# U and V rows of an expert slot fetched as one 8 KB row, and V rows added by VectorE and GpSimd instead of TensorE

## The reference

```python
best, pos = lax.top_k(cand, PEER_TOPK)
idx = jnp.take_along_axis(cand_idx, pos, axis=-1).reshape(T, PEER_HEADS * PEER_TOPK)
gate = jax.nn.softmax(best, axis=-1).reshape(T, PEER_HEADS * PEER_TOPK)
u_g = jnp.take(u_tab, idx, axis=0)
v_g = jnp.take(v_tab, idx, axis=0)
act = jax.nn.gelu(jnp.einsum('ted,td->te', u_g, xb).astype(jnp.float32)) * gate
return jnp.einsum('te,ted->td', act.astype(xb.dtype), v_g)
```

## Time and profile before

| | before |
|---|---|
| median of 3 runs | 3112.09 us (3095.13 to 3122.34) |
| the profiled execution | 3106.81 us, of which the span is 3105.0 us |
| PE busy | 2791.0 us (90%) |
| DVE busy | 1816.3 us (58%) |
| POOL busy | 1598.9 us (51%) |
| ACT busy | 699.8 us (23%) |
| DMA | 1006.77 MB, mean 324 GB/s |

### The profile page before, as it was taken

The page is one execution under the profiler, slowest core; times in us unless marked ns, Lnnn a source line. Parts: engine busy times, 40 slices in busy tenths (PEclk is TensorE's granted clock), DMA queues, the critical chain, the costliest instruction groups (busy, mean ns, idle before and its releaser), DMA issues.

```text
span 3105.0 us, 33154 instructions
## 1 busy us (share of the span) xinstructions
PE 2791.0 (90%) x11642; PEld 1607.6 (52%) x11642; DVE 1816.3 (58%) x4187; ACT 699.8 (23%) x1340; POOL 1598.9 (51%) x1334
## 2 busy tenths in 40 slices
PE   6999989688899979966699999999989999999997
PEld 4656647433334445534455555555555565555552
DVE  5331124775788746887466765555676755565552
ACT  4111122110104556657111111111111111111110
POOL 2111213274665544655566655565665756565654
PEclk9999999899999999988899999999999999999999
DMA  4332254397999999999999999999999999999997
GB/s 152 112 107 72 89 204 149 132 368 268 366 365 353 385 351 370 374 344 401 389 376 393 392 389 380 388 382 381 378 376 387 378 396 386 381 398 389 397 373 300
DMA packets 341676, 1006.77 MB, mean 324 GB/s; under 512 B 32295, under 2 KB 110887, under 8 KB 338952
## 3 DMA queue, kind: packets, MB, share of 16 engines
q0 software_dynamic: 184320, 671.17, 56.6%
q1 hardware_dynamic: 155464, 308.32, 28.1%
q10 hardware_dynamic: 1728, 25.17, 1.9%
HBM read 958.13 MB, written 46.40 MB: 324 GB/s over the span
## 4 chain that ended last, share of the span: by engine, by line
PE 50%; DMA 15%; issue 7%; DVE 4%; POOL 3%; SPq 1%; ACT 1%; another core or an unknown queue 0%; POOLq 0%; DVEq 0%; ACTq 0%
PE job_ps L1649 16%; PE v_ps L1673 7%; DMA v_rows<-in_peer_v,row_t 6%; PE wide_ps L128 4%; PE wide_ps L129 4%; PE wide_ps L130 4%; PE wide_ps L687 4%; PE job_ps L687 3%; DMA arena<-in_peer_ut 3%; DMA u_row<-in_peer_u,row_u 2%; PE gate_ps L687 2%; DMA arena<-in_peer_v 2%; DVE u_row L1908 1%; POOL u_row L1541 1%; POOL v_rows L1556 1%
## 5 line engine op out<-in xcount | busy, mean ns | idle before, releaser
L1556 POOL DMA_INDIRECT v_rows<-in_peer_v,row_t x622 | 705.7, 1135 | 718.0 <-PE v_ps L1673 561.6
L1908 DVE CUSTOM_DVE_ANT_0 u_row<-u_row,x_tile 128x1024 f32<-128x1024 f32 x640 | 776.3, 1219 | 295.2 <-DMA u_row<-in_peer_u,row_u 264.5
L1541 POOL DMA_INDIRECT u_row<-in_peer_u,row_u x640 | 758.1, 1185 | 289.0 <-issue 190.7
L1649 PE MATMUL job_ps<-arena 128*128 128x512 f32 x1536 | 702.7, 605 | 36.0 <-DVE arena L1968 23.8
L1649 PEld LDWEIGHTS job_ps<-arena 128*128 128x128 f32 x1536 | 288.7, 193 | 392.1 <-issue 339.0
L1673 PE MATMUL v_ps<-v_rows,picked 128*32 128x512 f32 x2488 | 368.0, 621 | 62.8 <-DMA v_rows<-in_peer_v,row_t 52.1
L128 PE MATMUL wide_ps<-x_hi,uw_lo 128*128 128x384 f32 x1024 | 375.4, 367 | 13.4 <-DVE uw_lo L1945 13.4
L129 PE MATMUL wide_ps<-x_lo,uw_hi 128*128 128x384 f32 x1024 | 343.9, 336 | 0.0
L130 PE MATMUL wide_ps<-x_hi,uw_hi 128*128 128x384 f32 x1024 | 343.8, 336 | 0.0
L957 POOL TENSOR_TENSOR exact<-arena,exact 128x1024 fp32r<-128x1024 f32 x48 | 116.3, 2427 | 434.3 <-ACT exact L699 434.3
L1784 ACT ACTIVATE uw_hi<-arena 128x1024 fp32r<-128x1024 f32 x128 | 135.1, 1056 | 720.8 <-DMA arena<-in_peer_ut 629.1
(11 more groups left out here) (302 smaller groups left out, 3060.5 us busy)
## 6 DMA issues: line engine op xcount, KB each, us to landing
arena<-in_peer_ut SPq DMA_DIRECT2D x128, 512.0 KB
arena<-in_peer_v SPq DMA_DIRECT2D x128, 512.0 KB
hand<-tmp_gates SPq DMA_DIRECT2D x32, 768.0 KB
tmp_gates<-arena ACTq DMA_DIRECT2D x10, 2048.0 KB
arena<-in_w_in SPq DMA_DIRECT2D x32, 512.0 KB, 3.7
hand<-in_w_in SPq DMA_DIRECT2D x32, 512.0 KB
x_tile<-tmp_xn SPq DMA_DIRECT2D x80, 128.0 KB
u_row<-in_peer_u,row_u POOLq DMA_INDIRECT x640
```

What stands on the lines that cost most here:

```text
L1541: pool.indirect_dma_start(u_row[n % NU][:], None, dram["peer_u"], bass.IndirectOffsetOnAxis(row_u[g % 2][:, e:e + 1], 0)).then_inc(u_in[n ...
L1556: pool.indirect_dma_start(v_row[b], None, dram["peer_v"], bass.IndirectOffsetOnAxis(row_t[g % 3][:, t:t + 1], 0)).then_inc(v_in[b], 16)
L1649: last = pe.matmul(job_ps[q % 2][:], actd[g % 2][:, jj, d * P:(d + 1) * P], vw[j % NO][:, half * 512:(half + 1) * 512], start=jj == 0, sto ...
L1908: dve.tensor_tensor_reduce(out=u_row[n % NU][:], in0=u_row[n % NU][:], in1=xb[h_ % 2][:], scale=1.0, scalar=0.0, op0=ALU.mult, op1=ALU.add ...
```

## The change

1. The host lays U and V side by side in one table `peer_uv` of 16,384 rows of 8 KB. One indirect DMA (`fetch`) brings 128 rows of 8 KB into one of 7 buffers `row`, and holds U and V for one expert slot of 128 tokens. `fetch_u`, `fetch_v`, the transposes of row numbers and gates and the reordering of tokens go; `xb` is one tile, loaded once per gathered tile (5 loads of 512 KB).
2. `pick`, `turn_act`, `keep_act`, `weigh` and `quad` go. For each slot, ScalarE does gelu of one column, multiplies it by the gate (one column), and scales the right half of V in place (512 wide). Three beats after the dot, VectorE does `add_side`: left half of V times the weight, added to `h`. GpSimd does `add_rest`: the scaled right half, added to `h`, seven slots behind the fetch, just before it reuses that buffer.
3. The dense V matmuls keep their sums in six PSUM banks over all 128 steps (`start=j == 0, stop=j == P - 1`); `sum_dense` runs six times at the end instead of 192 times. `vw` has 4 buffers instead of 6, `actd` holds two single steps.
4. One slot per beat all through: the dense pass starts at beat 240 and takes 3.046 beats a step. 

```diff
-            def fetch_u(n):
+            def fetch(n):
                 g, e = n // P, n % P
                 if e == 0:
                     pool.wait_ge(rows_u_done, g + 1)
-                if n >= NU:
-                    pool.wait_ge(dot_done, n - NU + 1)
-                pool.indirect_dma_start(u_row[n % NU][:], None, dram["peer_u"],
-                                        bass.IndirectOffsetOnAxis(row_u[g % 2][:, e:e + 1], 0)).then_inc(u_in[n % NU], 16)
+                if n >= NR:
+                    pool.wait_ge(added_side, n - NR + 1)
+                    pool.wait_ge(added_rest, n - NR + 1)
+                pool.indirect_dma_start(row[n % NR][:], None, dram["peer_uv"],
+                                        bass.IndirectOffsetOnAxis(row_u[g % 2][:, e:e + 1], 0)).then_inc(row_in[n % NR], 16)
+
+            def add_rest(n):
+                g, e = n // P, n % P
+                pool.wait_ge(scaled, n + 1)
+                if e == 0:
+                    pool.wait_ge(h_in[g % 2], 16 * (g // 2 + 1))
+                if n:
+                    pool.wait_ge(added_rest, n)
+                rest = h[g % 2][:, SIDE:D]
+                pool.tensor_tensor(rest, rest, row[n % NR][:, D + SIDE:2 * D], ALU.add).then_inc(added_rest, 1)
 
             pool.memset(p.a_pad, 0.0).then_inc(p.zeroed, 1)
-            for n in range(BEATS):
-                if n >= LAG:
-                    fetch_v(n - LAG)
-                for r in range(ROWS):
-                    if DOT_AT[r] == n:
-                        fetch_u(r)
+            for n in range(ROWS):
+                if n >= NR:
+                    add_rest(n - NR)
+                fetch(n)
+            for n in range(ROWS - NR, ROWS):
+                add_rest(n)
...
+            def gelu(n):
+                g, e = n // P, n % P
+                act.wait_ge(dot_done, n + 1)
+                act.activation(gelu_e[:, e:e + 1], dots[:, e:e + 1], ACT.Gelu_apprx_tanh).then_inc(gel_done, 1)
+                if e == 0:
+                    act.wait_ge(gate_done, SOFT.index(GATHERED[g]) + 1)
+                act.wait_ge(gel_done, n + 1)
+                act.activation(act_e[:, e:e + 1], gelu_e[:, e:e + 1], ACT.Copy,
+                               scale=gate_q[g % 2][:].rearrange("p h r -> p (h r)")[:, e:e + 1]).then_inc(act_done, 1)
+                act.wait_ge(act_done, n + 1)
+                rest = row[n % NR][:, D + SIDE:2 * D]
+                act.activation(rest, rest, ACT.Copy, scale=act_e[:, e:e + 1]).then_inc(scaled, 1)
...
+            def add_side(n):
+                g, e = n // P, n % P
+                dve.wait_ge(act_done, n + 1)
+                if e == 0:
+                    dve.wait_ge(h_in[g % 2], 16 * (g // 2 + 1))
+                if n:
+                    dve.wait_ge(added_side, n)
+                side = h[g % 2][:, 0:SIDE]
+                dve.scalar_tensor_tensor(out=side, in0=row[n % NR][:, D:D + SIDE], scalar=act_e[:, e:e + 1], in1=side,
+                                         op0=ALU.mult, op1=ALU.add).then_inc(added_side, 1)
...
+            def job(j):
+                pe.wait_ge(weighted, j + 1)
+                pe.wait_ge(vw_in[j % NO], 16 * (j // NO + 1))
...
+                for q in range(2 * ND):
+                    d, half = q // 2, q % 2
+                    last = pe.matmul(job_ps[q][:], actd[j % 2][:, d * P:(d + 1) * P], vw[j % NO][:, half * 512:(half + 1) * 512],
+                                     start=j == 0, stop=j == P - 1)
...
+                if n >= K:
+                    add_side(n - K)
+                if n < ROWS:
+                    dot(n)
                 route_on(n, 1)
```

More of the change, by code:

```diff
@@ L1272, in second_and_experts @@
     CHOSEN = {1: (40, 1), 4: (LAST + 1, 4), 5: (LAST + 8, 2)}
[L1273 to L1285, removed]
+    RANKED_AT = (-1, 51, 105, 143, LAST + 4, LAST + 13, LAST + 124, 494)
+    GATED_AT = (0, 58, 108, 147, LAST + 6, LAST + 20, LAST + 130, 502)
+    assert 191 < LAST and LAST + 20 < 2 * P - NR and LAST + 130 < 3 * P - NR and RANKED_AT[-1] < 4 * P - NR
+    X_AT = [P * g - 1 if g else 0 for g in range(NG)]
+    ADD_AT = [P * (g + 1) + K for g in range(NG)]
+    NORM_AT = [max(ADD_AT[g] + 4, LAST + 5) for g in range(NG)]
+    assert TURNED + 4 < X_AT[2] and all(NORM_AT[g] + 12 < P * (g + 2) for g in range(NG - 2))
     CHUNK_AT = [GATED_AT[2] + 3 + 3 * c for c in range(EARLY // 2)]
@@ L1351, in second_and_experts @@
         uw = [place(28 + 4 * b, D) for b in range(NW)]
-        vw = [place(kb, D) for kb in (40, 44, 48, 52, 88, 92)]
+        vw = [place(40 + 4 * b, D) for b in range(NO)]
         uw_lo = [exact(f"uw_lo{b}", 28 + 4 * b, D) for b in range(NW)]
@@ L1356, in second_and_experts @@
         gt = [place(6 * b, BLOCKS, GJ * 32) for b in range(2)]
-        actd = [place(76 + 6 * b, GJ, TD) for b in range(2)]
+        actd = [place(76 + 1.5 * b, TD) for b in range(2)]
         gain_f = place(60, D)
@@ L1511, in _ @@
                         load_dense(0, j)
-                    for j in range(GJ):
+                    for j in range(NO):
                         load_dense(2, j)
@@ L1680, in _ @@
             pre.step()
-            turn_rows(0)
             for n in range(END):
@@ L1807, in _ @@
             for n in range(END):
+                if 0 < n <= ROWS:
+                    gelu(n - 1)
                 if n == X_SPLIT:
@@ L1829, in _ @@
                         hot_relu(c)
-                for h_ in range(4 * NG):
-                    if n == GEL_AT[h_]:
-                        gelu(h_)
                 for g in range(NG - 1):
-                    if n == ADD_AT[g] + 2:
+                    if n == ADD_AT[g] + 1:
                         rms_root(g)
@@ L2069, in _ @@
                     jw += 1
[L2070 to L2080 removed]
+                if n >= K:
+                    add_side(n - K)
+                if n < ROWS:
+                    dot(n)
+                route_on(n, 1)
+            dve.wait_ge(acc_in, 16)
+            dve.wait_ge(job_done, P)
+            for q in range(2 * ND):
+                sum_dense(q)
+            dve.wait_ge(summed, 2 * ND)
             for d in range(ND):
```

360 lines of the change are left out of this document (86 added, 274 removed).

## The result

The changed kernel takes 3375.9 us (median of 4 runs, 3371.7 to 3382.1) against 3111.3 of the kernel before (4 runs, 3095.1 to 3122.3): a ratio of 1.086, 95% interval 1.081 to 1.091. The forecast was 3235 us, range 3050 to 3330. The direction was right, the size was not: the kernel is 265 us slower, not 123, and lies outside the range.

What follows compares the result with a forecast made beforehand. VectorE, locked out during GpSimd's additions, was to replace DMA as bound: 1872 us own work + 819 additions - 84 hidden + 25 idle = 2632, after an untouched 600, giving 3235 us, 4% slower; 80% range 3050 to 3330.

Steps and rivals of the forecast that it cites:

- What bounds it: After 600 us: VectorE, held up by GpSimd's additions, sets the pace at 2632 us; DMA, at 2423, no longer does.
- one pair of rows: Trace of the kernel before: a VectorE tensor-tensor beside a GpSimd addition took 2.74 us instead of about 0.69.
- The hidden share: GpSimd's additions that fall on VectorE's one-input work and hold nothing up: 10%, 84 us of 819.
- I take 25 us net: VectorE's idle time after 600 us, 910 us in the kernel before, adds only 25 us to its path.
- I cost it at nothing: ScalarE's in-order queue, the slot's gelu behind `uw_high`: no cost, as VectorE has three beats of slack, about 12 us.
- The rival I built: ScalarE's queue: a third of 93 `uw_high` waits overrun the slack by 5 us, 3385 us; within a rival of 10%.
- 8 KB rows save 60 us: DMA work after 600 us: one 8 KB row instead of two of 4 KB saves 60 us, between nothing and 140.
- The upper bound of 140 us: Most that 8 KB rows could save in DMA work: 27.4 ns on each of 81,920 rows over 16 engines.
- The DMA floor of 3030 us: Whole kernel if additions hide and DMA sets the pace: 600 + 2423 + 7 = 3030 us.
- "faster" rival: Nearly half of GpSimd's additions hide in VectorE's waits, DMA sets the pace: 3030 down to 2950 us; chance 20%.
- the likeliest case: The forecast itself, VectorE held up by GpSimd's additions: 3235 us, said to span 3150 to 3320; chance 58%.
- The third rival: ScalarE's queue delays VectorE, 3385 us, or 8 KB fetches cost POOL two descriptors, 3310 us; chance 10%.

Runs made afterwards that it cites:

- the two pairs of kernels above: Changed kernel with VectorE adding all of V, 8 KB rows against two 4 KB fetches: 3166.3, 3146.5 us; with ScalarE's slot work last: 3129.5, 3099.6 us.
- the two kernels: Against the changed kernel: VectorE adds all 1,024 columns of V, 3166.3 us; GpSimd's additions replaced by two memsets, 3134.7 us.

## Why the prediction was right in kind and wrong in size

Step by step, against its own terms:

| after 600 us | forecast | measured |
|---|---|---|
| VectorE's own work | 1872 | 1875 |
| blocked by GpSimd's additions | 819 - 84 = 735 | 672 |
| VectorE idle | 25 | 230 |
| sum | 2632 | 2777 |

- **What bounds it** was right: VectorE with GpSimd's lock, DMA at 0.89. VectorE's own work is right to 3 us, in part by luck: `add_side` at 742 ns instead of 0.70 us is 27 us more than I counted, and some 24 us elsewhere, which no run took apart, are less. That the two engines exclude each other came from one pair of rows and held.
- **GpSimd's addition**: 1.28 us forecast, 1.28 in the median, 1.32 in the mean, as now and then it is itself held by VectorE: one that starts at 1224.87 us, 0.14 us after a dot, takes 2.22.
- **The hidden share** was 20%, not 10%: 63 us less than forecast. That fits additions falling into the larger idle time, as less idle time came with more blocked time when ScalarE's order was changed.
- **The step that failed is "I take 25 us net" for VectorE's idle time.** It was 230 us. Idle and blocked time are coupled (less idle, more blocked), but not one for one: taking 130 us of idle time away shortened the profiled execution by 77. The term is short by 205 us. I wrote that idle time "shrinks but doesn't vanish" and then, of 910 us, kept next to none; it needed a row by row look at who would still be late.
- **Its cause is the step "I cost it at nothing" on ScalarE**, more than half of it: with the slot's work last the idle time is 100 us instead of 230. The rival I built had the slot's gelu late behind a waiting `uw_high`; that wait is 8 us in all. The reverse happened. The slot's three operations stand first in the beat, wait for the newest dot (ScalarE waits 1326 us for dots) and hold everything behind them: the dense gelu, `uw_high`, the mixer's copies. VectorE then waits for those. They take 0.20 + 0.29 + 0.72 = 1.22 us, not 1.0. Moving them to the end of the beat is worth 66 us; leaving out the 0.72 and keeping the order is worth 31. How the rest divides between the wait for the dot and the work itself, no run separates.
- **8 KB rows save 60 us**: of packet time they do save about that, of the kernel's time nothing. In the two pairs of kernels above the gather queue needs 1,026 and 708 engine-us less with 8 KB rows, 64 and 44 us on 16 engines, and the kernel with them is 20 and 30 us slower. In the changed kernel itself even the packet time isn't less: 52.6% of 16 x 3376.8 = 28,419 engine-us over 81,920 rows, 347 ns for 8 KB against 2 x 171.6 in the kernel before. It is 356 ns with 768 columns on GpSimd, 336 with 256, 333 with none; no run says why. The upper bound of 140 us had a slip besides: the line through 171.6 ns for 4 KB and 614.5 for 16 KB leaves 24.0 ns a row, not 27.4, so 123 us, and it was drawn between unlike queues. The Trainium skill (DMA: Bandwidth & Descriptors, "Anatomy of one DMA"), read as a price per fetch, had 2 us to gain on each slot; the runs disagree. (My 373 GB/s against it was of all transfers, not of the fetches alone.)
- **The DMA floor of 3030 us** that carried the "faster" rival doesn't exist. With the lock gone entirely, 3166 and 3135 us remain, since up to beat 240 the two kernels take 1041 and 1014 us where the one before took 901. VectorE is busy 916 us of the first and 801 of the second (654 before), so its own routing, mixer, dots and additions all but fill it in the first only; in the second VectorE's largest wait there is for ScalarE (61 us for routing scores). I had summed VectorE over 2505 us, where it has slack only in the last 1600. Here the two stretches have different bounds and their slacks don't add. The chance of 20% was too high; a forecast of the same kernel without GpSimd's additions would have been wrong in sign.
- **By stretch**: to dot 203 934 us (forecast 840), 203 to 240 197 (175), the rest 1646 (1615). 116 of the 147 us missed lie before beat 240, where ScalarE has the mixer and the gate matrices as well.
- **Part 3** was costed at 126.5 us and is worth 96 here: right in kind, less as the sums overlap in groups and are work that the lock doesn't touch.
- The range missed because its upper end allowed 30 us more of waits, where 205 came. Two slips in the arithmetic don't change that: 3232 + 1.8 + 5 is 3239, not 3235, and the terms named for the likeliest case span 3110 to 3297, not 3150 to 3320. Dots and `add_side` grew together by 0.36 + 0.42 = 0.78 us a slot, not 1.1. The third rival's 3385 is near the result by a mechanism that did not occur.

What stays open: the 100 us of idle time that remain with ScalarE's work last have no large owner in the waits (28.9 us for the weight, 23.8 us for rows, then smaller ones), and no run took them apart. Why the gather's packets take longer the more columns GpSimd adds, and why the row size moves the lateness from one queue to the other, is open too. Nor was it tried to place GpSimd's additions beside VectorE's one-input work.

No version beats the kernel before by a margin that counts: the best, 3099.6 us, has VectorE add all of V, 4 KB fetches and ScalarE's slot work last, at a ratio of 0.998. It keeps the change's simpler gather without its two costs.

## What to carry to other kernels

Work given to GpSimd that reads SBUF isn't parallel to VectorE's two-input work: count its duration on VectorE's path, less the share that meets one-input or PSUM-fed work, and compare with what VectorE needs to do it alone (here 0.53 us against 0.8 x 1.32 = 1.05). When a small step per iteration goes onto an in-order engine, ask not only whether it will be late but what it holds up while it waits for its newest input, and try it last in the iteration (66 us here). Make a floor by stretch, not by totals: a kernel with one bound up to beat 240 and another behind can't trade their slack. And a saving in an engine's busy time is no saving of the kernel's time: 8 KB rows saved packet time in both pairs, and the kernels with them were slower.
